# Four consecutive cached tokens per partition in the sample pages of a hybrid-attention decoder step

## The reference

```
past = (gather_pages(cache_cmp_kv[l], page_table), gather_pages(cache_sel_kv[l], page_table), state_win_kv[l],
        gather_pages(cache_diff_k[l], page_table), gather_pages(cache_diff_v[l], page_table))
```

## Time and profile before

| | before |
|---|---|
| median of 3 runs (lowest, highest) | 1460.26 us (1458.56, 1460.40) |
| the profiled execution | 1461.19 us |
| its span, first to last instruction | 1459.5 us |
| TensorE busy | 1389.9 us (95%) |
| VectorE, ScalarE, POOL busy | 473.1, 280.8, 106.1 us |
| DMA | 509.45 MB, 349 GB/s over the span |
| mean granted clock of TensorE | 0.993 |

### The profile page before, as it was taken

One profiled execution on the slowest core, in us unless ns is written; L12 is line 12 of the kernel. 1 busy time (PEld: TensorE's weight loads), 2 busy tenths in 40 slices (PEclk: granted clock), 3 DMA queues, 4 the chain that ended last, 5 costly groups with the idle time before them and its releaser, 6 DMA issues.

```text
span 1459.5 us, 19997 instructions
## 1 busy us (share of the span) xinstructions
PE 1389.9 (95%) x7350; PEld 614.5 (42%) x7350; DVE 473.1 (32%) x1110; ACT 280.8 (19%) x584; POOL 106.1 (7%) x217
## 2 busy tenths in 40 slices
PE   7999998989999999999999999999999999999987
PEld 3446554766674454333333333333333333333322
DVE  1114474545633653132122221331331322213314
ACT  2003343444533121000101101101001001011002
POOL 1000223325400000000000000000000000000000
PEclk9999999999999999999999999999999999999999
DMA  7334686799988769999999999999999999999996
GB/s 264 115 115 169 245 174 219 192 302 279 300 261 241 298 252 428 427 428 430 427 428 430 428 428 428 429 428 428 428 429 427 428 430 427 428 430 428 428 427 256
DMA packets 92878, 509.45 MB, mean 349 GB/s; under 512 B 19066, under 2 KB 37986, under 8 KB 67586
## 3 DMA queue, kind: packets, MB, share of 16 engines
q1 hardware_dynamic: 77602, 480.99, 82.3%
q0 software_dynamic: 15232, 27.89, 6.6%
HBM read 502.25 MB, written 10.62 MB: 351 GB/s over the span
## 4 chain that ended last, share of the span: by engine, by line
PE 75%; DMA 19%; ACT 2%; issue 2%; SPq 1%; DVE 1%; ACTq 0%; DVEq 0%
PE PS L1435 25%; PE PS L1465 11%; DMA arena<-in_w_gate_up 10%; PE PS L1409 6%; PE PS L352 5%; DMA arena<-in_w_down 4%; PE PS L2129 4%; PE PS L1401 4%; PE PS L1116 2%; PE PS L1297 2%; DMA arena<-in_cache_sel_kv 2%; PE PS L587 2%; PE PS L573 2%; DMA arena<-in_cache_diff_k 2%; PE PS L361 1%
## 5 line engine op out<-in xcount | busy, mean ns | idle before, releaser
L1435 PE MATMUL PS<-arena 128*64 128x512 f32 x2048 | 456.2, 595 | 13.9 <-DMA arena<-in_w_gate_up 12.9
L1435 PEld LDWEIGHTS PS<-arena 128*64 128x64 f32 x2048 | 141.5, 137 | 295.2 <-issue 263.1
L1465 PE MATMUL PS<-arena 128*64 128x512 f32 x1024 | 226.9, 594 | 2.3 <-DMA arena<-in_w_down 2.2
L1891 DVE TENSOR_SCALAR arena<-PS 128x512 f32<-128x512 f32 x32 | 22.1, 692 | 451.1 <-PE PS L1444 450.1
L1465 PEld LDWEIGHTS PS<-arena 128*64 128x64 f32 x1024 | 71.8, 137 | 150.5 <-issue 144.3
L1409 PE MATMUL PS<-arena 128*128 128x512 f32 (+1 forms) x180 | 84.2, 608 | 0.0
L1401 PE MATMUL PS<-arena 128*128 128x512 f32 (+1 forms) x192 | 79.4, 617 | 4.5 <-ACT arena L1601 3.7
L1258 POOL COPY arena<-arena 96x64 bf16 (+1 forms) x34 | 8.1, 240 | 996.0 <-PE PS L1472 944.7
L352 PE MATMUL PS<-arena 128*128 128x512 f32 (+1 forms) x192 | 78.9, 572 | 1.6 <-DMA arena<-in_w_in 1.6
L573 PE MATMUL PS<-arena 128*128 128x128 f32 (+1 forms) x456 | 67.8, 281 | 12.1 <-DMA arena<-in_cache_diff_k 5.5
L1812 DVE TENSOR_TENSOR arena<-PS,arena 128x512 f32<-128x512 f32 x32 | 21.8, 688 | 163.7 <-PE PS L1417 161.2
(11 more groups left out here) (293 smaller groups left out, 1279.4 us busy)
## 6 DMA issues: line engine op xcount, KB each, us to landing
arena<-in_w_gate_up SPq DMA_DIRECT2D x128, 2048.0 KB, 20.1
arena<-in_w_down SPq DMA_DIRECT2D x62, 2048.0 KB, 22.2
arena<-in_w_in SPq DMA_DIRECT2D x9, 2048.0 KB, 12.6
arena<-in_cache_diff_k SPq DMA_DIRECT2D x64, 256.0 KB, 6.8
arena<-in_cache_diff_v POOLq DMA_DIRECT2D x64, 256.0 KB, 8.7
arena<-in_cache_cmp_kv POOLq DMA_DIRECT2D x64, 128.0 KB, 5.6
arena<-in_cache_sel_kv SPq DMA_DIRECT2D x64, 128.0 KB, 7.9
arena<-in_state_win_kv SPq DMA_DIRECT2D x8, 512.0 KB, 8.6
```

Of the source, the lines that this page charges most:

```text
L1435: last = nc.tensor.matmul(bank(2 + role + 2 * u)[64 * h:64 * h + 64], hTm[:, k, BS * u:BS * u + BS], gu_w[:, k, D * role + 512 * h:D * rol ...
L1465: last = nc.tensor.matmul(bank(6 + u)[64 * h:64 * h + 64], aT[u][:, c % 4, 64 * (c // 4):64 * (c // 4) + 64], down_w[u][c // 4][:, c % 4, ...
```

## The change

Tokens of a page are laid out four to a partition: token 4p + r of a page stands in partition p (of 32), slot r. Four pages make a quad, page h of a quad taking the partitions 32h to 32h + 31. A DMA of one page now writes 32 partitions, with 8 KB to each for difference keys and values and 4 KB for selected pages. The window goes to 128 partitions with 4 KB to each. The number of DMAs and their bytes stay as they were, and so do the compressed pages. As a page now lies in the slots of all four chunks of its quad, the first page of a quad waits until all four chunks are transposed. The masks follow the new order; the drop mask is added in two instructions. `dv_raw`, `winT` and `selT` move, the copies of `win0` and `win1` first wait for the last gate store, and `gates1` is loaded directly after `gates2`.

```diff
+RUN = 4
-    a["oldw"] = np.where(np.arange(NT)[None] > t[:, None], 0, NEG)
+    a["oldw"] = np.where(np.arange(NT).reshape(NT // RUN, RUN).T.reshape(1, NT) > t[:, None], 0, NEG)
...
-        dv_raw = [[at(6144 + 512 * j, 512) for j in range(NPAGE)],
-                  [at(34304 + 512 * j if j < NPAGE - 1 else 30720, 512) for j in range(NPAGE)]]
+        dv_raw = [at(6144, NPAGE, 512), at(33792, NPAGE, 512)]
...
-        winT, selT = at(31232, 2, WIN), at(32256, 2, PAST)
+        winT, selT = at(30720, 2, WIN), at(31744, 2, PAST)
...
+        def in_runs(raw, quad, h):
+            rows = PAGE // RUN
+            return raw[rows * h:rows * h + rows, RUN * quad:RUN * quad + RUN, :]
+        def page_runs(pool_d, page):
+            return pool_d[bass.ds(page, 1)].rearrange("a (p r) n -> (a p) r n", r=RUN)
...
-                            sp.dma_start(sel_raw[:, b, 4 * k + h],
-                                         sel_d[bass.ds(pages[b][4 * k + h], 1)].rearrange("a p n -> (a p) n")).then_inc(sel_in[2 * b + k], 16)
+                            sp.dma_start(in_runs(sel_raw[:, b], k, h), page_runs(sel_d, pages[b][4 * k + h])).then_inc(sel_in[2 * b + k], 16)
...
-                    sp.dma_start(win_raw[:, b], win_d[bass.ds(2 * i + b, 1)].rearrange("a (s p) n -> p (a s) n", p=128)).then_inc(win_in[b], 16)
+                    sp.dma_start(win_raw[:, b], win_d[bass.ds(2 * i + b, 1)].rearrange("a (p r) n -> (a p) r n", r=RUN)).then_inc(win_in[b], 16)
...
-                    if first and b:
-                        past(sp, l_tp, pg + 1)
-                    elif not first:
-                        past(sp, l_tp, i * L_TP + (NPAGE - L_TP + group_at(f"nk{pg}" if b else f"kd{pg}") + 1))
-                    sp.dma_start(dk_raw[:, pg], kd_d[bass.ds(page, 1)].rearrange("a p n -> (a p) n")).then_inc(dk_in[pg // 4], 16)
+                    if pg % RUN == 0:
+                        if first and b:
+                            past(sp, l_tp, pg + RUN)
+                        elif not first:
+                            past(sp, l_tp, i * L_TP + (NPAGE - L_TP + group_at(f"nk{pg + RUN - 1}" if b else f"kd{pg + RUN - 1}") + 1))
+                    sp.dma_start(in_runs(dk_raw, pg // RUN, pg % RUN), page_runs(kd_d, page)).then_inc(dk_in[pg // 4], 16)
...
-                    pool.dma_start(dv_raw[b][pg], vd_d[bass.ds(page, 1)].rearrange("a p n -> (a p) n")).then_inc(dv_in[2 * b + pg // 4], 16)
+                    pool.dma_start(in_runs(dv_raw[b], pg // RUN, pg % RUN), page_runs(vd_d, page)).then_inc(dv_in[2 * b + pg // 4], 16)
...
+                gates_stored(eng, 11)
                 st(copy(winT[:, int(name[3]), :], src), done)
...
-                mid = s_old[:, SB:SB + n14 * SB].rearrange("p (a b) -> p a b", b=SB)
-                st(V.tensor_tensor(mid, mid, dropm.unsqueeze(2).to_broadcast([128, n14, SB]), ALU.add))
+                drop = dropm.rearrange("p (q b) -> p q b", q=2)
+                for q in range(2):
+                    quad = s_old[:, 512 * q:512 * q + 512].rearrange("p (r b n) -> p r b n", r=RUN, n=SB // RUN)
+                    st(V.tensor_tensor(quad, quad, drop[:, q].unsqueeze(1).unsqueeze(3).to_broadcast([128, RUN, 8, SB // RUN]), ALU.add))
...
-            load(sp, "gates2", gsig[0:ROWS[2], 2], gate_pre[0:ROWS[2], 4 * D:6 * D])
-            past(sp, l_pv, PAIRS_OF_SEQ * VALUES + (PV_D1 - VALUES))
-            load(sp, "gates1", gsig[0:ROWS[1], 1], gate_pre[0:ROWS[1], 2 * D:4 * D])
+            for t in (1, 2):
+                load(sp, f"gates{t}", gsig[0:ROWS[t], t], gate_pre[0:ROWS[t], 2 * D * t:2 * D * t + 2 * D])
```

More of the change, by code:

```diff
@@ L92, in shape_constants @@
     a["half"] = (p[:, None] % 32 // 16 == np.arange(2)[None])
-    a["blk"] = np.tile(np.arange(1, PAST // SB - 1), (128, 1))
+    blk = np.arange(PAST // SB)
+    a["blk"] = np.tile(np.where((blk == 0) | (blk == PAST // SB - 1), -1, blk), (128, 1))
     d = {}
@@ L222, in build @@
         TILE_ORDER = (2, 0, 1)
-        pgs, mass, imp, dropm = alloc(NCC + 1), alloc(14, 4), alloc(14), alloc(14)
+        pgs, mass, imp, dropm = alloc(NCC + 1), alloc(14, 4), alloc(14), alloc(16)
         smx, primer = alloc(8), alloc(16)
@@ L647, in dif_values @@
                             if j < NPAGE:
-                                nc.tensor.matmul(out, ptl[:, j, 32 * h:32 * h + 32], dv_raw[b][j][:, 128 * h:128 * h + 128], start=(j == 0), stop=False)
+                                nc.tensor.matmul(out, ptl[:, j, 32 * h:32 * h + 32], dv_raw[b][:, j, 128 * h:128 * h + 128], start=(j == 0), stop=False)
                             else:
@@ L814, in build @@
         ACT_PER_TURN = {"l_out_act": 19, "l_gelu": 2, "l_exp": 4, "l_sq": 1, "l_root": 1}
-        DVE_PER_TURN = {"l_out_dve": 14, "cmp_turned": 16, "l_dve": 42, "l_nmx": 4, "l_pn": 1, "l_sum": 1, "l_osm": 1, "l_on": 1, "l_var": 1,
+        DVE_PER_TURN = {"l_out_dve": 14, "cmp_turned": 16, "l_dve": 43, "l_nmx": 4, "l_pn": 1, "l_sum": 1, "l_osm": 1, "l_on": 1, "l_var": 1,
                         "l_odn": 1}
@@ L936, in turn @@
                 st.own()
-                st(V.scalar_tensor_tensor(imp, imp, lcf[:, 5:6], const("blk"), ALU.is_equal, ALU.mult))
+                st(V.scalar_tensor_tensor(imp, imp, lcf[:, 5:6], const("blk")[:, 1:n14 + 1], ALU.is_equal, ALU.mult))
                 st.own()
@@ L960, in turn @@
                 negmax(2, s_key)
-                st(V.tensor_tensor(s_win[:, 0:NT], s_win[:, 0:NT], const("oldw"), ALU.add))
+                oldest = s_win[:, 0:WIN].rearrange("p (r n) -> p r n", r=RUN)[:, :, 0:NT // RUN]
+                st(V.tensor_tensor(oldest, oldest, const("oldw", RUN, NT // RUN), ALU.add))
                 st.own()
```

## The result

The changed kernel takes 1510.8 us (1503.1 to 1515.2, 4 runs) against 1460.3 us: 1.035 times as long, 95% interval 1.032 to 1.038. That is 50 us more, where +4.5 was forecast. The time lies outside the range (1450 to 1487), and even above the time of rival 1 (1489), in which the two halves never overlap. The profiled execution is the shortest of the four, with 1503.1 us and a span of 1501.5, so the profiles show 42 us of the difference.

What follows compares the result with a forecast made beforehand. It took TensorE and the DMA engines, both nearly full, as the bound, with 10 us to win. 4 + 0 + 0.5 + 0 = +4.5 us on 1461.2 gave 1465.7, less 0.9 to the median, so 1465; range 1450 to 1487.

Steps and rivals of the forecast that it cites:

- rival 1: Two queues' loads to opposite partition halves never overlap, 215 GB/s only: +29 us, so 1489 us; chance 0.20.
- What bounds the kernel: Sample attention: TensorE and DMA engines nearly full; faster pages can win 6.8 us of waits, perhaps 3.4 of clock: 10.
- Price of the new destination: Loads to 32 partitions: 215 GB/s for one queue; two queues 215 in one half, 383 in opposite ones, mean 275.
- Share of the queues: Beside difference values, larger rows raise SP's share of the two queues' rate to one half, 137 GB/s.
- Middle turns: Two boundaries: waits for whole quads and queued bytes make SP's selected pages late; +2 us each, +4 in all.
- First and last turn: Quads and selected pages in the sample attention's first and last turns: 0 and +0.5 us booked.
- Clock: Lowered clock behind waits in the last and perhaps first turn: a possible gain of 2 x 1.7 = 3.4 us.
- Edits on other engines and the waits: Drop mask (+1.2 us at most), gate store wait, gates1 and window: 0 booked; whole-quad waits counted at the middle boundaries.
- Signs to look for: Profile after: both queues about 275 GB/s at 246 to 252 us, SP's share half; a middle turn over 55 us means rival 1.

Runs made afterwards that it cites:

- spread version: Changed kernel with page h of a quad in partitions h, h+4, h+8 and so on, drop mask in four additions: 1452.5 us, 0.9959 of the kernel before.
- values_only: Changed kernel with only POOL's values in quads, keys and selected pages back in rows on 128 partitions, waits for whole quads kept: 1503.4 us, ratio 1.031.
- other_edits: Changed kernel with key, selected and value loads put back in rows on 128 partitions, all other edits kept: 1460.9 us, ratio 1.0011.
- waits_only: Kernel before with nothing but the waits for whole quads (first key page of four waits for the fourth transposition): 1460.5 us, ratio 1.0013.

## Why the prediction was wrong

**What bounds the kernel.** Right: the rows named the DMA engines as full and TensorE's waits as small, and put the possible gain at 10 us at most. The spread version got 5 or 6 of it.

**Price of the new destination.** For one queue right: 215 GB/s was taken, and 203 to 223 measured. For two queues it failed, and this is the first step that did. It took 383 as the rate in opposite halves, from a row in which both queues had 128 partitions, and averaged to 275. Loads alone give 242 in opposite halves and 207 in one, and the kernel ran at 219 to 228. The average was between a measured end and one that nothing supported, and rows 7 spoke against it. Rival 1, to which 0.20 was given, had the rate nearly right.

**Share of the queues.** A half was taken for SP. In the changed kernel's first turn SP got 0.50 of 1.37 MB, 36%, or 83 GB/s instead of 137. At 83 GB/s the quad's 1.05 MB take 12.6 us instead of 7.7, and the wait for it grew from 2.19 to 9.25 us, where no growth was booked. The half itself came from an alternation by packets, read from rows 12. With both queues in the lower half loads alone keep to it (734 packets of q1 to 699 of q0, half of the bytes each), but the first turn does not: in the view of 246 to 252 us q0 got 156 packets and q1 81. Why is open. What the step also left out is that a slow packet of one queue delays the other, as `values_only` shows.

**Middle turns.** Here is the term that was mis-sized most: +2 for each boundary, 8.75 in rival 1, and +12.3 and +17.3 measured. The rate is one part of it. The other is that the sum priced the bytes from the last key page to `sel3`, 24 us of a turn, and left the rest at its old pace. But the rest had held the room to spare, with 285 and 186 GB/s in the kernel before at 324 to 331 and 331 to 340 us:

```profile
DMA packets 1104, 1.99 MB, mean 285 GB/s; under 512 B 114, under 2 KB 147, under 8 KB 1104
...
DMA packets 1378, 1.68 MB, mean 186 GB/s; under 512 B 938, under 2 KB 938, under 8 KB 1378
```

At some 219 GB/s the bytes of a turn fill all of that room and 12 us more. One division, of a whole turn's bytes by the rate, shows both parts. With the measured rate it is 13.7 MB / 219 GB/s = 62.6 us, between the two turns measured (60.8 and 65.5). With rival 1's 215 it is 63.7 us, so that rival 1 would have come to some 42 us and not 29. With the forecast's own 275 it is only 49.8 us, 1.3 above the old turn: the wrong rate alone was enough to hide the loss. And once everything is late, other loads are waited for: the window three times with over 1 us, the values once with 5.09, both booked at nothing.

**First and last turn.** 0 and +0.5 booked, +6.4 and +6.7 measured. Rival 1 had 4 and 7.5.

**Clock.** The forecast counted the clock only as a possible gain. Behind the new waits it fell, to 0.90, 0.92, 0.87 and 0.92 over the four stretches against 0.96, 1.00, 1.00 and 0.97, and TensorE's busy time grew by 9.7 us. This cost was booked at nothing.

**Edits on other engines and the waits.** Right: `other_edits` and `waits_only` put both at 0.1%, and no more than 0.3% by the intervals. The mask took two additions of 690 ns each, as booked:

```profile
L970 DVE TENSOR_TENSOR PS<-PS,arena x8: 690/690/690, 287.6 to 473.2; 128x512 f32<-128x512 f32 x8
```

**Signs to look for.** The view of 246 to 252 us fell to 228, which is nearer rival 1's 215 than 275. SP's share beside values did not rise to half in that view, and the middle turns passed the 55 us that the prediction had named as rival 1's sign.

## What to carry to other kernels

Before a load is cut to fewer partitions for longer rows, check which partitions it keeps: here 32 neighbours gave 203 to 223 GB/s and every fourth one 389, with the same rows. If a stage keeps the DMA engines as busy as this one (a share of 0.96), divide all of its bytes by the new rate; the stretch around the wait that binds today is too small a piece. And the layout of one queue's load is not a matter of that queue alone: with only the values narrow, it was the loads of the other queue that came late, and the kernel lost 3.1%, where it lost 3.5% with all three loads narrow.

## What the runs showed of the hardware

A narrow load drags a wide one: 221 GB/s together against 388 for two wide ones, and in one window of `values_only` 33 GB/s were left for 1 KB rows beside it. Opposite halves on two queues move 17% more than one half (242 against 207 GB/s).

The kernel before has slow stretches of its own, with its compressed pages (rows 11). Their layout was tried in loads alone, one stretch of one run for each case. The turned layout (token 4k + r to partition 32r + k) runs at 95 GB/s on SP's queue with 27% of 16 engines' time, which is about four engines' worth (0.27 x 16 = 4.3). The Trainium skill (DMA: Bandwidth & Descriptors, "Why a DMA increments its semaphore by 16 and not by 1") says that a DMA runs on the largest number of engines, up to 16, that divides the slowest dimension of both sides. These are 4 in the source and 128 in the destination here, so 4; the row agrees. On POOL's queue, where the kernel has these loads, the same layout alone runs at 180 GB/s, and with a token to a partition at 235. Beside key pages the turned pages pull both queues to 220 GB/s, or to 273 with the keys spread; with a token to a partition instead, it is 375. A layout of the compressed pages without that outer 4 would be the next thing to try in the kernel; no run here did.
